# First norm, turn and first products by blocks of 128 tokens, and the small row loads spread between the first weight units

## What is computed

```
def first_block(x, attn_norm, w_in, ...):
    h = rmsnorm(x, attn_norm)                  # x: 256 x 1024, float32
    proj = h @ w_in                            # 1024 x 3592
    mq, mk, mv, gqkv, gz, ga, gb = split(proj) # attention, gated delta rule, gates
    ...
def rmsnorm(x, gain):
    return x * rsqrt(mean(x * x, axis=-1) + 1e-6) * gain
...
def second_block(x, ...):
    h = modulate(rms_norm(x, norm1), ...)
    p = h @ w_in_2                             # its columns 512 to 767 (k and v of attention A) come first
```

## Time and profile before

| | us |
|---|---|
| median of 3 runs | 814.06 |
| lowest, highest | 813.48, 814.84 |
| the profiled execution, its own time | 814.7 |
| span of its trace | 812.9 |

### The profile page before, as it was taken

How to read it: one execution, slowest core, us unless ns; L and a number is a source line. 1 busy time by engine, 2 the same in 40 slices (tenths; PEclk the granted TensorE clock), 3 DMA queues, 4 the chain that set the end, 5 groups by cost and what they waited for, 6 DMA issues and landing times. The chain is left out here.

```text
span 812.9 us, 14120 instructions
## 1 busy us (share of the span) xinstructions
PE 748.1 (92%) x5753; PEld 545.6 (67%) x5753; DVE 444.3 (55%) x770; ACT 322.1 (40%) x554; POOL 45.4 (6%) x33
## 2 busy tenths in 40 slices
PE   8999999899998987778877899799999999999998
PEld 5978976554744754544644687466547888888886
DVE  3899755554542232122131796657467766577565
ACT  4667433410442232232241844467532533433431
POOL 1000021010000000000000033500000000000000
PEclk9999999999999999999899999899999999999999
DMA  8894459979899999999999994600008444565201
GB/s 287 291 347 157 154 206 401 340 274 383 317 370 395 414 421 417 410 422 417 414 415 398 387 275 168 206 1 2 1 9 301 140 173 156 197 228 196 104 1 52
DMA packets 106308, 208.24 MB, mean 256 GB/s; under 512 B 7910, under 2 KB 55303, under 8 KB 98319
## 3 DMA queue, kind: packets, MB, share of 16 engines
q1 hardware_dynamic: 105326, 205.25, 67.8%
q10 hardware_dynamic: 864, 2.18, 0.8%
q0 software_dynamic: 64, 0.05, 0.0%
HBM read 206.38 MB, written 1.08 MB: 255 GB/s over the span
## 5 line engine op out<-in xcount | busy, mean ns | idle before, releaser
L2653 DVE TENSOR_TENSOR unit_parts<-ring,unit_parts 128x2048 fp32r<-128x2048 f32 x33 | 75.6, 2290 | 57.7 <-ACT unit_parts L1973 57.7
L1973 ACT ACTIVATE unit_parts<-ring 128x2048 fp32r<-128x2048 f32 x33 | 62.9, 1912 | 73.9 <-PE psa L1335 43.0
L1334 PE MATMUL psv<-column_parts,unit_parts 128*128 128x512 f32 (+1 forms) x192 | 65.5, 389 | 1.6 <-DVE arena L2735 1.4
L1037 PE MATMUL psv<-ring,arena 128*32 128x256 f32 x976 | 57.9, 380 | 8.9 <-DMA ring<-in_w_up_dram 8.9
L1334 PE MATMUL psa<-column_parts,unit_parts 128*128 128x512 f32 (+1 forms) x192 | 65.1, 387 | 0.0
L1037 PEld LDWEIGHTS psv<-ring,arena 128*32 128x32 f32 x976 | 33.7, 110 | 30.0 <-issue 11.2
L2778 POOL TENSOR_TENSOR small<-small,consts 128x2 f32<-128x2 f32 (+4 forms) x15 | 26.3, 1754 | 461.8 <-DVE small L2497 243.7
L1335 PE MATMUL psv<-column_parts,unit_parts 128*128 128x256 f32 (+1 forms) x192 | 52.0, 271 | 0.0
L1335 PE MATMUL psa<-column_parts,unit_parts 128*128 128x256 f32 (+1 forms) x192 | 52.0, 271 | 0.0
L1786 ACT ACTIVATE arena<-psv 128x256 f32<-128x256 f32 x8 | 3.1, 384 | 102.1 <-PE psv L1037 102.1
L1334 PEld LDWEIGHTS psv<-column_parts,unit_parts 128*128 128x128 f32 x192 | 36.1, 188 | 9.3 <-DVE unit_parts L2653 1.5
(11 more groups left out here) (440 smaller groups left out, 1684.5 us busy)
## 6 DMA issues: line engine op xcount, KB each, us to landing
ring<-in_w_gate_dram SPq DMA_DIRECT2D x43, 1024.0 KB, 9.3
ring<-in_w_up_dram SPq DMA_DIRECT2D x40, 1024.0 KB, 5.1
arena<-in_w_down_dram SPq DMA_DIRECT2D x32, 1024.0 KB
ring<-in_w_mod_dram SPq DMA_DIRECT2D x24, 1024.0 KB, 7.4
ring<-in_w_in_dram SPq DMA_DIRECT2D x23, 1024.0 KB, 10.1
ring<-in_w_down_dram SPq DMA_DIRECT2D x11, 1024.0 KB, 7.2
ring<-in_w_out_dram SPq DMA_DIRECT2D x8, 1024.0 KB, 8.6
arena<-in_w_in_dram SPq DMA_DIRECT2D x8, 512.0 KB, 17.2
```

Of the source, the lines that this page charges most:

```text
L1037: mm = pe.matmul(mG[32 * e:32 * e + 32, f0:f0 + FF], XT[:, k, 32 * e:32 * e + 32], w, start=(k == 0), stop=(k == KD - 1))
L1334: pe.matmul(both_parts(bank, t_0, t_1), hi, col_parts[:, :, k, t_0:t_1], start=(k == 0), stop=False)
L1973: act.activation(unit_parts[q % 3][:, 0, :], slot_of(NPRE + u_), ACT.Copy).then_inc(upper_done, 1)
L2653: vec.tensor_tensor(lo, slot_of(NPRE + at["mlp"] + 3 * n + kind), hi, ALU.subtract).then_inc(lower_done, 1)
```

## The change

- TensorE, VectorE, ScalarE and GpSimd handle the first norm by blocks. The power is taken of one column at a time, `rows_normed` is counted up for each block, and each block is turned by `turn_block` and emptied by `turned_block` as four chunks of 128 tokens to a bank.
- VectorE empties the first block's bank before it prepares and scales the second block.
- The products of unit 0 are 32 of 128 tokens instead of 16 of 256. The eight of the first 128 columns of weights and the first block come first, then the turns of the second block, then the other 24. They wait by halves of a block: for VectorE's bank at chunk 0, and for ScalarE's at chunk 4.
- The second run of `keep_busy` has 4 products instead of 6.
- SyncE issues unit 2 right behind units 0 and 1, unit 3 behind the fourth of the small transfers that follow, unit 4 behind the eighth, and unit 5 behind the last.
- In the second block the products of `unit_ka` wait by halves in the same way.
- The numbers of `power_done` and `rows_normed` go up by one from there on.

```diff
@@ TensorE
-            keep_busy(PSX[1], 6)
+            keep_busy(PSX[1], 4)
             pe.wait_ge(rows_normed, 1)
-            turn(hn)
-            pe.wait_ge(v_free, nv)
-            pe.wait_ge(a_free, na)
+            turn_block(hn, 0)
+
+            def cols_T_first():
+
+                bank = PSA[2]
+                w = unit(1)[0]
+                for b in range(NB):
+                    for cc in range(2):
+                        for k in range(KD):
+                            if cc == 0 and k in (0, 4):
+                                pe.wait_ge(*((a_free, 1 + b) if k else (v_free, 2 + b)))
+                            mm = pe.matmul(bank[:, cc * T + b * P:cc * T + b * P + P], w[:, k, cc * P:(cc + 1) * P],
+                                           hT[:, k, b * P:(b + 1) * P], start=(k == 0), stop=(k == KD - 1))
+                        if (b, cc) == (0, 0):
+                            pe.wait_ge(rows_normed, 2)
+                            turn_block(hn, 1)
+                assert a_bank() is bank
+                mm.then_inc(a_ready, 1)
+                freed.append((a_ready, na))
+
...
-            cols_T()
+            cols_T_first()
             cols_T()
...
             for b in range(NB):
-                pe.wait_ge(v_free, at["t", b][0])
-                pe.wait_ge(a_free, at["t", b][1])
                 bank = a_bank()
                 for kk in range(KD):
+                    if kk % 4 == 0:
+                        pe.wait_ge(*((a_free, at["t", b][1]) if kk else (v_free, at["t", b][0])))
                     mm = pe.matmul(bank[:, 0:256], hTx[:, kk, b * P:(b + 1) * P], unit_ka[:, kk, :],
@@ SyncE
                 if name == "attn":
-                    stream(0, 2)
+                    stream(0, 3)
+                if name in ("on_b", "c_ctx"):
+                    stream(*{"on_b": (3, 4), "c_ctx": (4, 5)}[name])
             sp.dma_start(brow[:], v("b_mod_2").rearrange("l (n c) -> (l n) c", c=P)).then_inc(s_rows, 16)
-            stream(2, 6)
+            stream(5, 6)
@@ ScalarE
-            turned(hT, vc[:, ROWS["attn"]:ROWS["attn"] + KD])
+            for b in range(NB):
+                turned_block(hT, b, vc[:, ROWS["attn"]:ROWS["attn"] + KD])
@@ VectorE
-            normed(xres, hn)
+            def row_block(b):
+
+                nonlocal nsq
+                nsq += 1
+                dve.wait_ge(squares_done, nsq)
+                rsqrt(ss[:, b:b + 1], rstd[:, b:b + 1], D)
+                vec.tensor_scalar(hn[:, b, :], xres[:, b, :], rstd[:, b:b + 1], None, ALU.mult).then_inc(rows_normed, 1)
+
+            attn = vc[:, ROWS["attn"]:ROWS["attn"] + KD]
+            row_block(0)
             dve.wait_ge(v_free, 1)
-            turned(hT, vc[:, ROWS["attn"]:ROWS["attn"] + KD])
+            turned_block(hT, 0, attn)
+            row_block(1)
+            turned_block(hT, 1, attn)
             dve.wait_ge(pad_done, 1)
@@ GpSimd
-            power(rstd)
+            for b in range(NB):
+                power(rstd[:, b:b + 1])
```

More of the change, by code:

```diff
@@ L71 @@
 PAIRS_A = (0, 5, 1, 4, 2, 7, 3, 6)
-ROUTE_POWER = 4
-HEAD_POWERS = (12, 13)
+ROUTE_POWER = 5
+HEAD_POWERS = (13, 14)
 MOD_LEVELS, MOD_DELTA, MOD_LAST = (0, 1, 2, 3, 4, 5, 6, 7), (8, 9, 10), 11
@@ L972, in ctx_b @@
                 mm.then_inc(ctx_ready, 1)
-            pe.wait_ge(rows_normed, 2)
+            pe.wait_ge(rows_normed, 3)
             turn_pair(hnc, 0, a_bank()).then_inc(a_ready, 1)
@@ L992, in _ @@
             pe.matmul(bank[:, 0:NE], c("ones"), sel[:, 1, :], start=False, stop=True).then_inc(v_ready, 1)
-            pe.wait_ge(rows_normed, 3)
+            pe.wait_ge(rows_normed, 4)
             pe.wait_ge(a_free, na)
@@ L1100, in _ @@
             for b in range(NB):
-                pe.wait_ge(rows_normed, 4 + b)
+                pe.wait_ge(rows_normed, 5 + b)
                 turn_block(hnx, b)
@@ L1301, in _ @@
             freed2.extend([(halves_ready, 6)] * 2)
-            pe.wait_ge(rows_normed, 6)
+            pe.wait_ge(rows_normed, 7)
             turn_block(hnx, 0)
@@ L1355, in up_first @@
                         if b == 0 and kind == 0:
-                            pe.wait_ge(rows_normed, 7)
+                            pe.wait_ge(rows_normed, 8)
                             turn_block(hnx, 1)
@@ L1571, in turned, with turned_block @@
                     ins.then_inc(a_free, 1)
+            def turned_block(dst, b, scale, shift=None):
+                bank = a_take()
+                for kk in range(4):
+                    k = 4 + kk
+                    d_, b_ = dst[:, k, b * P:(b + 1) * P], bank[:, kk * P:(kk + 1) * P]
+                    if shift is None:
+                        ins = act.activation(d_, b_, ACT.Copy, scale=scale[:, k:k + 1])
+                    else:
+                        ins = act.activation(d_, b_, ACT.Identity, scale=scale[:, k:k + 1], bias=shift[:, k:k + 1])
+                ins.then_inc(a_free, 1)
             for b in range(NB):
@@ L1823, in _ @@
             act.wait_ge(moe_sums_added, 4 * trips)
[L1824 to L1834, removed]
             def upper2(n):
@@ L2057, in _, with turned_block @@
             vec.tensor_copy(vc[:, 0:KD], bank[:, 0:KD]).then_inc(v_free, 1)
-            normed(xres, hn)
+            def turned_block(dst, b, scale, shift=None):
+                bank = v_take()
+                for k in range(4):
+                    d_, b_ = dst[:, k, b * P:(b + 1) * P], bank[:, k * P:(k + 1) * P]
+                    if shift is None:
+                        ins = vec.tensor_scalar(d_, b_, scale[:, k:k + 1], None, ALU.mult)
+                    else:
+                        ins = vec.tensor_scalar(d_, b_, scale[:, k:k + 1], shift[:, k:k + 1], ALU.mult, ALU.add)
+                ins.then_inc(v_free, 1)
+            def row_block(b):
[6 more added lines that the diff above has]
+            row_block(0)
             dve.wait_ge(v_free, 1)
-            turned(hT, vc[:, ROWS["attn"]:ROWS["attn"] + KD])
+            turned_block(hT, 0, attn)
+            row_block(1)
+            turned_block(hT, 1, attn)
             dve.wait_ge(pad_done, 1)
@@ L2480, in _ @@
             dve.wait_ge(moe_sums_added, 4 * trips)
[L2482 to L2491, removed]
             dve.wait_ge(parts_squared, 4 * trips)
```

## The result

The changed kernel takes 817.86 us (816.65 to 819.49, six runs) against 814.21 us for the kernel before beside it (812.83 to 814.84, six runs): a ratio of 1.0048, 95% interval [1.0032, 1.0064]. It is slower by 0.5%, where 813.0 us was forecast. The profiled execution took 816.65 us, its span 814.9 us. It is the fastest of the six, and its mean granted clock, 0.989, the highest (0.982 to 0.989). So the traces of the two kernels are only 1.95 us apart (814.70 and 816.65), and the medians 3.65.

A forecast was written before the change was run, and what follows sets the result against it. TensorE, busy 92% of the span, was taken as the bound. 1.0 us from the beginning plus up to 0.1 from the second block made 1.05, so 814.06 - 1.05 = 813.0 us; range 811.8 to 814.4.

The forecast's parts named there:

- The beginning: Chain to unit 0's first product: it starts at 10.4 instead of 12.71, the small rows' turn 1.0 us earlier.
- The rival in which they are dear: Unit 0's half-wide products cost up to 0.434 us each, net 5.5 slower; with 0.32 each, 816.0; chance 0.03.
- the estimate of 0.32 us: Cost of one half-wide product by the skill page's weight-load rule; small rows' turn at 28.6; the prediction's rows contradicted it.
- The transfers: SyncE's loads from 12 us: hole closes, later landings 2 us earlier, convolution near 29; no gain itself, protects the 1.0.
- The small rows had no DMA as a releaser; that rival: The small rows' data land late, at about 28.4, and TensorE waits: net 1.8 slower, 815.9; chance 0.05.
- the rival in which TensorE follows VectorE: Behind the convolution the stages go by VectorE, whose chain starts 2 us earlier: gain 2.0, 812.0; chance 0.15.
- The second block: `unit_ka`'s products start some 0.8 us earlier, but the split products behind wait for VectorE: gain 0, at most 0.1.
- The clock: Rival: the clock falls at the beginning, as the slow first idle products suggested; net 0.3 slower, 814.4; chance 0.05.
- what it starts earlier it ends earlier: From the first product until well past 100 us TensorE runs nearly without holes, so an earlier start is kept.
- What TensorE pays for it: Unit 0: 32 half-wide products take 7.35 us where 16 took 6.95, 0.4 lost; the second block's turns add 0.9.
- Gone at 450: Sign of being wrong: the 1.0 us is there at 100 us and gone, or doubled, at 450.
- The rival in which the gain is lost among the experts: The experts' stage starts by transfers that don't move, so the time is 814.1; chance 0.12.

The follow-up runs named there:

- after_plus144_again: The changed kernel with 144 TensorE instructions of fill in its idle products at the beginning, measured once more: 813.36 us, ratio 0.999.
- before_plus200: The kernel before with 200 TensorE instructions of fill, as narrow idle products at the beginning: 814.92 us, ratio 1.001.
- after_plus84: The changed kernel with 84 TensorE instructions of fill in its first run of idle products: 817.05 us, ratio 1.0034.
- after_plus28: The changed kernel with 28 TensorE instructions of fill in its first run of idle products: 819.95 us, ratio 1.0075.
- after_plus144: The changed kernel with 144 TensorE instructions of fill in its idle products at the beginning, first run: 813.54 us, ratio 0.9995.

## Why the prediction was wrong

**The beginning** was right in its times. The argument was put at 6.6 (6.58), the scaling done and the turns at 8.2 (8.26), unit 0's first product at 10.4 (10.31), the second block's turns at 12.2 (12.17) without a hole, ScalarE's bank begun at 9.4 (9.46). The half-wide products were 0.23 each, as in the earlier trace rows: 5.52 us for 24 with the last one's end. The rival in which they are dear falls, and with it the estimate of 0.32 us. The small rows' turn came 1.3 us earlier and not 1.0: the first product began 0.1 earlier than put, and the 32 half-wide products took 7.22 us and not 7.35 (10.31 to 12.17 and 13.04 to 18.40). Two terms of the chain were off and nearly made up for each other: scaling began 0.87 us behind the argument and not 0.81, and VectorE's and ScalarE's four copies took 1.12 and 1.14 us and not 1.36 and 1.51. One condition was never looked at: unit 0 has to be there. It landed at 9.53, 0.8 us ahead of the first product. In `after_plus144_again` it landed at 10.17, and the first product, at 10.21, waited for it.

**The transfers** were right. The hole at 12 us is closed, the gates' unit was used at 27.93 and the convolution at 28.87, where "near 29" was said. That this edit gains nothing by itself but protects the gain is borne out by both single runs: alone it gives 0.9999, and without it the first small product is at 109.96 instead of 108.53. The wait for VectorE's part is 0.5 us of that, 0.4 was late from the start, and the rest is not traced to a cause. The small rows had no DMA as a releaser; that rival falls. So does the rival in which TensorE follows VectorE: VectorE's chain starts 2.1 us earlier and TensorE's 1.2.

**The second block** was right. `unit_ka`'s products start 2.21 us after the turns (457.54 and 459.75) and not 2.89 (455.23 and 458.12 before), 0.68 earlier. The split products that follow stand 9.72 us after the turns in both kernels. After:

```profile
459.75 7.14 PE L1129 MATMUL psa<-ring,arena 128*128 128x256 f32 x32 [0.24 <-DVE arena L2086]
...
467.26 0.50 PE L544 MATMUL psa<-in_upper,token_parts 128*128 128x512 f32 x1 [0.37 <-DVE ring_lower L2540]
```

What starts earlier now waits 0.37 us for VectorE's lower part: 0, as said.

**The clock** did not fall at the beginning, but for the first time at 128.0 us, which no rival had. That the slow first idle products were a matter of the clock, as this rival had it, isn't shown: the profile gives a granted clock of 1.00 for each microsecond from 1 us on, though its first record of the clock begins only at 3.9 us.

**The step that failed** is the first one, "what it starts earlier it ends earlier", which was argued for the time until well past 100 us and then carried on to the end. The gain was there at 109 us, 1.2 of it. In the next 66 us the changed kernel lost 4.1. The prediction counted the 16 added products as 0.4 us of work; they are also 64 instructions less the 8 of the two idle products, and that moved every border of the stage behind them. The term "What TensorE pays for it" has a second part, which was put at nothing without a reason and measured 4.1 us. "Gone at 450" stood among the signs of being wrong, but with no mechanism behind it. The rival in which the gain is lost among the experts had another place: with the borders at the same instructions (`before_plus200` and `after_plus144_again`) VectorE does the same work 1.6 us earlier at 190 to 255 us and 1.8 us earlier from 526 us to the end, so that nothing of it is lost there.

**The change itself.** With the borders of both kernels on the same instructions (place 200) it takes 813.36 us against 814.92, 1.56 less. Of this 0.8 is the beginning of the kernel before, which its own fill made late (first small product at 110.47 and not 109.70). Against the untouched kernel before the ratio is 0.999 [0.9981, 0.9999], 0.8 us, and the first run of the same kernel had 0.9995 [0.9985, 1.0005]. The fill of 200 gave 0.9993 [0.9984, 1.0002]. So at places without the loss the change is 0.4 to 0.8 us faster than the untouched kernel before, where 1.05 was forecast, and only one of the three intervals leaves out 1. The trace of `after_plus144_again` says the same: 1.2 us ahead at the first small product, and a stage of 66.7 us instead of 66.2, which leaves 0.7. At place 56 too the changed kernel (ratio 1.0048) stands below the kernel before with 56 of fill (1.0082). The best kernel of this study is the changed one with 144 or 200 instructions of fill at its beginning, 813.2 to 813.5 us; its lead over the kernel before is at the edge of what can be told.

**What stays open.** Why some transfers of instructions start 3.7 us after the last border and others 5.8 (126.53 to 132.29 in the table of borders); what two executions of `after_plus84` did otherwise; whether the falls of the clock in the stage are brought about by the stalls. It fell there in four of the six kernels with stalls over 0.5 us, before 156 us, and in none of the seven others; but `after_plus84` stood still for 3.8 us without it.

## What to carry to other kernels

Instructions added or taken away anywhere move everything behind them against the borders of TensorE's instruction blocks, and a stage of many small products can pay several us for that, with no engine named as its releaser. So when a small edit at the beginning costs time far behind it, look for idle time with "issue" as its cause, number TensorE's records there, and repeat the edit with 50, 100 and 200 instructions of fill before judging it. And compare two kernels at the same place of the borders: beside the untouched kernel before, the same change reads as 0.5% slower without fill and as 0.1% faster with it.

## What the runs showed of the hardware

- A queue of its own brings 16 KB at a time, which by the spacing of the stalls is 256 of TensorE's instructions, and in 13 profiled executions all stalls without a releaser over 0.5 us in the stage of small products stand within four records of a border.
- At a stall TensorE goes on 1.2 to 1.5 us after such a transfer has ended. The shortest time between two borders of this stage was 5.55 us in any of the kernels; a transfer took 0.9 to 1.0 us, beside DMA engines at a share of 1.05 (up to 1.4 us in `after_plus28` and `after_plus84`).
- The loss isn't bounded by the stalls, and a border isn't always a loss: the longest stall was 2.3 us, and in `after_plus144` two borders among products of 512 columns brought no idle time, only 0.5 us more for one of the two runs. The changed work took 66.7 to 75.6 us for the same stage, and the worst place (84) spent 13.7 us of it at 1.2 GHz.
- TensorE's idle products at the beginning can be many, if they are narrow: 45 and 16 pieces of about 40 and 64 columns brought the first small product to 109.43, as many of 28 and 56 columns to 108.20, against 108.53 without fill.
- Products also have idle time "issue" that belongs to no border: L1091 (L1074 before) stands still five times for 0.56 us among the experts, in both kernels, at the same products. A stall that stays with its product is another thing than one that stays with the border.
